# A three-pass fp32 transformer kernel: matmul order in the paired product, and one weight split moved ahead of a sigmoid

## The chip, the cores and the metric
One core of a Trainium2 chip runs the whole program. The metric is the device time of one execution in microseconds (us); lower is better.

## The reference
Four transformer layers over 256 tokens of width 1024, in fp32. Layer 0 mixes tokens by latent attention, layer 1 by dilated attention, layers 2 and 3 by a mixture of retention, block attention and a short convolution. Each layer ends with a gated feed-forward network of inner width 2816. Layers 0 and 1 then add a second, gated input. What matters here, cut down:

```
def swiglu(h, w_in, w_out):
    gu = h @ w_in                       # 1024 -> 2 x 2816
    return (jax.nn.silu(gu[..., :D_FF]) * gu[..., D_FF:]) @ w_out
...
h = h + rms_norm(swiglu(rms_norm(h, g[2]), ffn_w_in[i], ffn_w_out[i]), g[3])
h = h + (p[i] @ ple_w_proj[i]) * jax.nn.sigmoid(h @ ple_w_gate[i])   # layers 0 and 1
```

In layers 2 and 3 the feed-forward network has a short convolution and a GELU in the place of the SiLU.

## The kernel before
**Precision by three products.** Every fp32 operand is held as a high part and a low part (`w_hi` and `w_lo`, `xt_hi` and `xt_lo`), both as fp32r. A product is hi x hi + hi x lo + lo x hi, summed in PSUM.

**The stream of weights.** All weights come from HBM in chunks of at most 128 x 2048 numbers, numbered c through the whole program, into six slots (`SLOTS`). SP issues the load of chunk c when chunk c - 6 has been used (`chunk_used`). ScalarE makes the high part of each (L1057, `hi_part`), GpSimd subtracts it to get the low part (L440), and TensorE waits for that (`lo_split`) before its first matmul on the chunk. ScalarE has other work too, so its program says by hand where the high parts are made: `ahead(c, LEAD)` makes all high parts up to chunk c + 4 that are not made yet. An engine takes its instructions in the order written, so whatever stands behind a waiting high part waits too.

**The paired product** (`paired_product`, L547 to L558) computes 256 features of the feed-forward input (128 of each of its two matrices) from one chunk. There are 22 such chunks in a layer; the first three (layers 0 and 1) or four (layers 2 and 3) are computed in another way, the rest by `paired_product`. It has two halves of 128 features, one PSUM bank each. `xt_both` holds the high and the low part of the activations side by side, so one wide matmul of 512 columns gives hi x hi and hi x lo; a narrow one of 256 columns adds lo x hi to the first 256 columns. With eight pieces of the contraction (`kt`), a half has 8 wide and 8 narrow matmuls. Before, they run as 7 wide, 8 narrow, 1 wide. Every matmul has a weight load of its own.

**The end of layers 0 and 1** (`ple`). The gate projection has four chunks (C_GATE to C_GATE + 3), the second input's projection has one (C_PROJ = C_GATE + 4), and the next stage starts at C_GATE + 5. Rows are in two blocks of 128 tokens, tb 0 and tb 1. TensorE's order is: the first three gate chunks for tb 0 and for tb 1, the fourth for tb 0 (`gate0_ready`), the projection for tb 0 (`y0_ready`), the fourth gate chunk for tb 1 (`chunk_used`), the transposes of `h` for tb 0 (L617), the projection for tb 1, and then the next layer's first products. ScalarE takes the sigmoid of each block from PSUM into `t1` (L1177); VectorE multiplies the projection by it (L1659) and adds it to `h` (L1660), half a row block at a time; the transposes wait for each half (`rows_ready`).

**ScalarE's part before:** the high parts up to C_GATE + 6, then the wait for `gate0_ready` and the first sigmoid, then the high part of C_GATE + 7 (this is the third chunk of the next stage), then the wait for the second sigmoid.

Of the kernel before, what the change touches and what calls it, by code (L numbers as in the profile page):

```python
# [20 lines left out]
KT = D // P  # L21
# [6 lines left out]
LEAD = 4  # L28
# [24 lines left out]
PROJ_N, FFN_OUT_N = KT // 2, FT // 2  # L53
# [28 lines left out]
C_GATE = tuple(c + FFN_OUT_N for c in C_OUT[:2])  # L82
# [62 lines left out]
def build(nc, x, pT, positions, inv_freq, gain_fm, gain_rows, onehot, rel_table, rel_table_2, causal, decay,  # L145
# [7 lines left out]
    with ctx:  # L153
        def sb(name, shape, dt=F32, at=ctx):
            return at.enter_context(nc.sbuf_tensor(name, shape, dt))
# [11 lines left out]
        xt_both = sb("xt_both", [P, 2, KT, SEQ], F32R)  # L167
        xt_hi, xt_lo = xt_both[:, 0], xt_both[:, 1]
# [277 lines left out]
        def _(pe):  # L446
            def mm(dst, lhsT, rhs, start, stop):
                return nc.tensor.matmul(dst, lhsT, rhs, start=start, stop=stop)  # L448
# [13 lines left out]
            def chunk(c, cols):  # L462

                if c >= C_MLA:
                    pe.wait_ge(lo_split, c + 1 - C_MLA)
                s = c % SLOTS
                n = W // cols
                return (w_hi[:, s, 0:n * cols].rearrange("p (k n) -> p k n", n=cols),
                        w_lo[:, s, 0:n * cols].rearrange("p (k n) -> p k n", n=cols))
# [77 lines left out]
            def paired_product(c, banks):  # L547

                hi, lo = chunk(c, 2 * P)
                for half in range(2):  # L550
                    f = slice(half * P, (half + 1) * P)
                    both = psum[:, banks[half], :].rearrange("p (a t) -> p a t", a=2)
                    for kt in range(KT - 1):
                        mm(both, hi[:, kt, f], xt_both[:, :, kt, :], kt == 0, False)
                    for kt in range(KT):
                        mm(both[:, 0], lo[:, kt, f], xt_hi[:, kt, :], False, False)
                    ins = mm(both, hi[:, KT - 1, f], xt_both[:, :, KT - 1, :], False, True)
                ins.then_inc(chunk_used, 1)  # L558

            def wide_chunk(c, m, n, lhs, at, down=False, second=lambda: None):  # L560
# [68 lines left out]
            def ffn(l):  # L629

                t = T_FFN[l]
                held = BEGUN[t]

                def hidden_tile(u):
                    k = u - held
                    if k > 0:
                        pe.wait_ge(hidden_ready, l * FT + (1, held)[k - 1] if k < LANES else l * FT + u - LANES + 1)
                    paired_product(C_IN[l] + u, PAIRS_AT[k % LANES])

                def then():  # L640
                    if l < 2:
                        turn_r((2, 4)[l], t)
                    hidden_tile(held)

                begin_tiles(t, C_IN[l], then)
                for u in range(held + 1, FT):
                    hidden_tile(u)
                for m in range(FFN_OUT_N - HOLD):
                    pe.wait_ge(hidden_ready, l * FT + 2 * m + 2)
                    wide_chunk(C_OUT[l], m, FFN_OUT_N, (ht_hi, ht_lo), y_at("out", l),  # L650
                               second=(lambda: pe.wait_ge(hidden_ready, l * FT + FT - 2)) if m == 0 else lambda: None)
                pe.wait_ge(hidden_ready, l * FT + FT)
                wide_end(C_OUT[l], FFN_OUT_N, (ht_hi, ht_lo), y_at("out", l), (T_PLE0, T_PLE1, T_MIX3, None)[l], l >= 2)
# [282 lines left out]
            for l in (2, 3):  # L936
# [32 lines left out]
                for f in range(RH):  # L969
                    for tb in range(TB):  # L970
                        off = 2 * BANK + f * SEQ + tb * P
                        ins = nc.tensor.transpose(flat[:, off:off + P], ret[:, tb, f * P:(f + 1) * P], ident[:, :])
# [6 lines left out]
                for hh in range(RH):  # L979
# [3 lines left out]
                    ins = mm(logits[:, hh, far], q[:, P:SEQ], k, True, True)  # L983
# [7 lines left out]
                for hh in range(RH):  # L991
# [3 lines left out]
                    ins = mm(logits[:, hh, far], k[:, 0:P], q, True, True)  # L995
# [6 lines left out]
                for hh in range(RH):  # L1002
# [4 lines left out]
                    ins = mm(psum[:, 3, o], dec[:, hh, near], v[1], False, True)  # L1007
# [3 lines left out]
                for j in range(3 * RH):  # L1011
# [3 lines left out]
                    ins = nc.tensor.transpose(flat[:, off:off + P], sc2[:, j // 3, (j % 3) * P:(j % 3 + 1) * P], ident[:, :])  # L1015
# [7 lines left out]
                for hh in range(RH):  # L1023
# [4 lines left out]
                    ins = mm(flat[rows, off + P:off + SEQ], mvr[:, 1, hh, :], probT2[:, 3 * hh + 2, :], False, True)  # L1028
# [22 lines left out]
        def _(act):  # L1051
            def hi_part(c):

                s = c % SLOTS
                act.wait_ge(landed[s], 16 * (c // SLOTS + (1 if s >= C_MLA else 0)))
                width = WIDTHS[c]
                nc.scalar.activation(w_hi[:, s, 0:width], raw[:, s, 0:width], ACT.Copy).then_inc(hi_split, 1)  # L1057
# [3 lines left out]
            def ahead(c, lead=2):  # L1061

                while begun[0] < min(c + lead + 1, CHUNKS):
                    hi_part(begun[0])
                    begun[0] += 1
# [34 lines left out]
            def border(t, y, c, normed):  # L1100

                held = BEGUN.get(t, 0)

                for tb in range(TB):
                    if y is not None:
                        y_squares(y, tb)
                    if tb == 1:
                        ahead(c, LEAD)
                        copy_rows(t, 0, range(held - 2))
                    turn_hi_block(t, xt_hi, tb)  # L1110
                    if normed:
                        act.wait_ge(rows_ready, rows_of(t, tb, 1))
                        h_squares(tb)
                ahead(c + 1, LEAD)
                copy_rows(t, 0, range(max(held - 2, 0), held))
                ahead(c + 2, LEAD)
                copy_rows(t, 1, range(held if t == T_DIL else min(held, 2)))
# [48 lines left out]

            def ple(l, then):

                for m in range(PROJ_N - 1):
                    ahead(C_GATE[l] + m, LEAD)  # L1170
                for tb in range(TB):
                    if tb == 0:
                        act.wait_ge(gate0_ready, l + 1)
                    else:
                        ahead(C_GATE[l] + PROJ_N - 1, LEAD)
                        act.wait_ge(chunk_used, C_PROJ[l])
                    nc.scalar.activation(t1[:, tb, :], flat[:, 2 * tb * BANK:(2 * tb + 2) * BANK],  # L1177
                                         ACT.Sigmoid).then_inc(sig_ready, 1)
                border(then, None, C_PROJ[l], then == T_DIL)
# [141 lines left out]
            load_gain(2, 0)  # L1321
            ffn(0)
            ple(0, T_DIL)
            load_gain(3, 1)

# [74 lines left out]
            load_gain(4, 0)  # L1400
            ffn(1)
            ple(1, T_MIX2)
            load_gain(5, 1)


            for l in (2, 3):
# [8 lines left out]
                for b in range(3):  # L1415
# [4 lines left out]
                    for tb in range(TB):  # L1420
                        src = psum[:, b % 2 + 2 * tb, :]
                        if b < 2:
                            ins = nc.scalar.activation(ret[:, tb, b * BANK:(b + 1) * BANK], src, ACT.Copy)
                        else:
                            nc.scalar.activation(ret[:, tb, 2 * BANK:3 * RW], src[:, 0:split], ACT.Copy)
                            ins = nc.scalar.activation(ret[:, tb, 3 * RW:], src[:, split:], ACT.Silu)
                    ins.then_inc(ret_copied, 1)
                for b in range(3):
                    ahead(c + 6 + b, LEAD - 1)
                    act.wait_ge(chunk_used, c + 7 + b)  # L1430
                    ins = nc.scalar.activation(mqk[:, b].rearrange("p a t -> p (a t)"), psum[:, 5 + b, :], ACT.Copy)
# [8 lines left out]
                for tb in range(TB):  # L1440
                    ins = nc.scalar.activation(mvr[:, tb, :, :].rearrange("p h d -> p (h d)"), psum[:, tb, 0:RW], ACT.Copy)
# [3 lines left out]
                for m in range(2 * RH):  # L1445
                    part = sc2[:, m % RH, near if m < RH else far]
                    ins = nc.scalar.activation(part, part, ACT.Exp, bias=nmax[:, m:m + 1], accum_out=rsum[:, m:m + 1])
# [645 lines left out]
```

## Time and profile before

| | |
|---|---|
| median of 3 runs | 1490.85 us (1490.66 to 1492.28) |
| profiled execution, its own time | 1492.28 us |
| its span in the profile | 1490.5 us |
| granted TensorE clock | 0.997 of full speed |
| busy: TensorE, GpSimd, ScalarE, VectorE | 97%, 71%, 48%, 44% |

Rows give times from the start of the span. PE is TensorE's matmuls and PEld its weight loads, DVE is VectorE, ACT is ScalarE, POOL is GpSimd, SPq the DMA issues of SP. The length of a matmul in the rows overlaps with its neighbours', so the pace of a stream is read from the starts.

### The profile page before, as it was taken

The numbers are of one execution on the slowest core, as the hardware profiler recorded it, in microseconds if no ns is written. First come the engines' busy times: TensorE is split into PE (matmuls) and PEld (weight loads), VectorE is DVE, ScalarE is ACT, GpSimd is POOL, SyncE is SP. The second block draws the span as 40 slices with busy tenths as digits, with TensorE's granted clock in tenths as the row PEclk, the third lists the DMA queues.
The fourth block names the chain that finished last, engine by engine and source line by source line (L and its number), as shares of the span: only waits on it lengthen the run. The fifth ranks groups of instructions, "written<-read, shape, count | busy, mean of one in ns | idle before, by whom it ended". The sixth has DMA issues, their size and how long they took to land.

```text
span 1490.5 us, 22190 instructions
## 1 busy us (share of the span) xinstructions
PE 1452.9 (97%) x9070; PEld 1291.8 (87%) x9070; DVE 651.9 (44%) x1346; ACT 714.8 (48%) x920; POOL 1058.4 (71%) x262
## 2 busy tenths in 40 slices
PE   7899999999999999999999999999999999999997
PEld 6788888889999999888888889889888899898885
DVE  5545545033322222345541335646660475556613
ACT  6775555344544444465544345535443346255540
POOL 4366988965566665568888668768889577678891
PEclk9999999999999999999999999999999999999999
DMA  6475555545554554435555465336556555355560
GB/s 224 160 279 194 177 191 197 191 165 193 177 180 160 176 172 159 170 118 208 197 184 189 167 249 199 123 137 213 188 197 221 185 207 190 123 198 187 183 224 29
DMA packets 64670, 271.19 MB, mean 182 GB/s; under 512 B 6122, under 2 KB 28832, under 8 KB 37953
## 3 DMA queue, kind: packets, MB, share of 16 engines
q1 hardware_dynamic: 39596, 242.22, 46.9%
q10 hardware_dynamic: 24981, 27.61, 5.5%
q8 instruction: 72, 1.18, 0.3%
q14 instruction: 21, 0.17, 0.0%
HBM read 268.68 MB, written 8.21 MB: 186 GB/s over the span
## 4 chain that ended last, share of the span: by engine, by line
PE 91%; DVE 5%; ACT 2%; issue 1%; DMA 0%; SPq 0%; DVEq 0%
PE psum L448 87%; PE psum L617 1%; PE psum L864 1%; DMA h<-x 0%; PE psum L526 0%; ACT prob L1274 0%; DVE prob L1763 0%; DVE newton L1509 0%; DVE psum L1668 0%; DVE psum L1678 0%; ACT xt_both L1075 0%; DVE nmax L1765 0%; DVE xt_both L1593 0%; ACT probT L1280 0%; DVE rstd L1512 0%
## 5 line engine op out<-in xcount | busy, mean ns | idle before, releaser
L440 POOL TENSOR_TENSOR w_lo<-raw,w_hi 128x2048 fp32r<-128x2048 f32 (+2 forms) x248 | 1045.0, 4230 | 391.9 <-ACT w_hi L1057 391.5
L1057 ACT ACTIVATE w_hi<-raw 128x2048 fp32r<-128x2048 f32 (+2 forms) x248 | 433.5, 1754 | 146.8 <-DMA raw<-w_tail 88.3
L448 PE MATMUL psum<-xt_both,w_hi 128*128 128x512 f32 (+1 forms) x2272 | 498.0, 341 | 0.8 <-DVE dqk L1811 0.8
L448 PEld LDWEIGHTS psum<-xt_both,w_hi 128*128 128x128 f32 x2272 | 382.1, 190 | 44.9 <-issue 6.0
L448 PE MATMUL psum<-w_hi,xt_both 128*128 128x256 f32 (+3 forms) x1328 | 318.4, 329 | 1.4 <-DVE xt_both L1593 1.4
L448 PE MATMUL psum<-xt_both,w_lo 128*128 128x256 f32 x1728 | 318.9, 282 | 0.0
L448 PEld LDWEIGHTS psum<-xt_both,w_lo 128*128 128x128 f32 x1728 | 265.6, 191 | 11.6
L448 PEld LDWEIGHTS psum<-w_hi,xt_both 128*128 128x128 f32 x1328 | 229.1, 190 | 18.1 <-issue 3.8
L448 PE MATMUL psum<-w_lo,xt_both 128*128 128x256 f32 (+3 forms) x664 | 211.0, 326 | 0.0
L448 PEld LDWEIGHTS psum<-w_lo,xt_both 128*128 128x128 f32 x664 | 126.1, 190 | 7.1
L1145 ACT ACTIVATE lanes<-lanes 128x256 f32<-128x256 f32 x88 | 36.8, 418 | 166.6 <-DVE lanes L1630 107.9
L448 PE MATMUL psum<-w_hi,ht_hi 128*128 128x512 f32 x352 | 108.7, 390 | 0.0
L448 PE MATMUL psum<-w_lo,ht_hi 128*128 128x512 f32 x352 | 108.5, 389 | 0.0
L448 PE MATMUL psum<-w_hi,ht_lo 128*128 128x512 f32 x352 | 108.3, 389 | 0.0
L1619 DVE TENSOR_TENSOR psum<-psum,rest 128x512 f32<-128x512 f32 x74 | 51.8, 700 | 108.8 <-ACT rest L1142 108.8
L448 PEld LDWEIGHTS psum<-w_lo,ht_hi 128*128 128x128 f32 x352 | 66.1, 188 | 13.8
L448 PEld LDWEIGHTS psum<-w_hi,ht_lo 128*128 128x128 f32 x352 | 66.1, 188 | 13.8
L448 PEld LDWEIGHTS psum<-w_hi,ht_hi 128*128 128x128 f32 x352 | 65.9, 188 | 13.3
L1142 ACT ACTIVATE rest<-psum 128x512 f32<-128x512 f32 x74 | 43.4, 587 | 50.4 <-PE psum L448 50.4
L1352 ACT ACTIVATE prob<-prob,nmax 128x384 f32<-128x384 f32 (+1 forms) x32 | 24.7, 773 | 67.5 <-DVE nmax L1824 67.5
L1668 DVE SCALAR_TENSOR_TENSOR psum<-h,psum 128x1024 f32<-128x1024 f32 x8 | 9.8, 1229 | 106.7 <-PE psum L448 106.6
L1562 DVE TENSOR_TENSOR psum<-psum,gbuf 128x512 f32<-128x512 f32 x16 | 11.1, 695 | 100.3 <-ACT lanes L1083 100.3
(212 smaller groups left out, 1389.2 us busy)
## 6 DMA issues: line engine op xcount, KB each, us to landing
raw<-w_tail SPq DMA_DIRECT2D x156, 1024.0 KB, 4.9
raw<-w_dil SPq DMA_DIRECT2D x24, 1024.0 KB, 4.9
raw<-w_mix SPq DMA_DIRECT2D x24, 1024.0 KB, 5.0
raw<-w_dil SPq DMA_DIRECT2D x16, 576.0 KB, 3.7
bias_tiles<-bias_rows ACTq DMA_DIRECT2D x1, 6912.0 KB
gbuf<-gain_rows ACTq DMA_DIRECT2D x12, 512.0 KB, 5.0
dbias<-bias_tiles ACTq DMA_DIRECT2D x16, 384.0 KB, 6.1
raw<-w_dil SPq DMA_DIRECT2D x8, 384.0 KB, 4.5
```

The costliest lines, as they stand in the source:

```text
L440: nc.gpsimd.tensor_tensor(w_lo[:, s, 0:width], raw[:, s, 0:width], w_hi[:, s, 0:width].bitcast(F32), ALU.subtract).then_inc(lo_split, 1)
L448: return nc.tensor.matmul(dst, lhsT, rhs, start=start, stop=stop)
L617: ins = nc.tensor.transpose(psum[:, bank, n * P:(n + 1) * P], src[:, tb, kt * P:(kt + 1) * P], ident[:, :])
L864: ins = nc.tensor.transpose(flat[:, 5 * BANK + j * P:5 * BANK + (j + 1) * P], prob1[:, j * P:(j + 1) * P], ident[:, :])
L1057: nc.scalar.activation(w_hi[:, s, 0:width], raw[:, s, 0:width], ACT.Copy).then_inc(hi_split, 1)
L1142: nc.scalar.activation(rest[:, k], psum[:, first:first + 2, SEQ:2 * SEQ], ACT.Copy).then_inc(rest_ready, 1)
L1145: nc.scalar.activation(gate[:, u % LANES, :], conv[:, u % LANES, :], func).then_inc(gate_ready, 1)
L1352: nc.scalar.activation(prob1[:, part], prob1[:, part], ACT.Exp, bias=nmax[:, qb:qb + 1], accum_out=rsum_q[:, qb, hh:hh + 1]).then_inc(d_ex ...
L1562: return v.tensor_tensor(rows[:, cols], rows[:, cols], gbuf[:, slot, cols], ALU.mult)
L1619: step(v.tensor_tensor(both, both, rest[:, k], ALU.add))
L1668: step(v.scalar_tensor_tensor(rows, h[:, tb, :], ALPHA, rows, ALU.mult, ALU.add))
```

## The change
In `paired_product` the wide and the narrow matmuls of a half alternate by `kt`, and the last wide one stays last. In ScalarE's part of `ple` the high part of chunk C_GATE + 7 moves from behind the first sigmoid to ahead of the wait for it.

```
--- before
+++ after
@@ paired_product (TensorE)
-                    for kt in range(KT - 1):
-                        mm(both, hi[:, kt, f], xt_both[:, :, kt, :], kt == 0, False)
                     for kt in range(KT):
-                        mm(both[:, 0], lo[:, kt, f], xt_hi[:, kt, :], False, False)
-                    ins = mm(both, hi[:, KT - 1, f], xt_both[:, :, KT - 1, :], False, True)
+                        if kt < KT - 1:
+                            mm(both, hi[:, kt, f], xt_both[:, :, kt, :], kt == 0, False)
+                        ins = mm(both[:, 0], lo[:, kt, f], xt_hi[:, kt, :], False, False)
+                    ins = mm(both, hi[:, kt, f], xt_both[:, :, kt, :], False, True)
@@ ple (ScalarE)
-                for m in range(PROJ_N - 1):
+                for m in range(PROJ_N):
                     ahead(C_GATE[l] + m, LEAD)
                 for tb in range(TB):
                     if tb == 0:
                         act.wait_ge(gate0_ready, l + 1)
                     else:
-                        ahead(C_GATE[l] + PROJ_N - 1, LEAD)
                         act.wait_ge(chunk_used, C_PROJ[l])
```

PROJ_N is 4, KT is 8, TB is 2.

## Rows read from the trace of the kernel before

**Rows 1.** The page: busy times, and the chain that ended last by engine.

```profile
PE 1452.9 (97%) x9070; PEld 1291.8 (87%) x9070; DVE 651.9 (44%) x1346; ACT 714.8 (48%) x920; POOL 1058.4 (71%) x262
...
PE 91%; DVE 5%; ACT 2%; issue 1%; DMA 0%; SPq 0%; DVEq 0%
```

**Rows 2.** Groups of instructions by shape, TensorE; busy us, mean ns of one.

```profile
L448 PE MATMUL psum<-xt_both,w_hi 128*128 128x512 f32 x1184 | 298.5, 393 | 0.0
```

**Rows 3.** Timeline of paired halves, layer 0, TensorE: start, length, what.

```profile
202.25 1.11 PE L448 MATMUL psum<-xt_both,w_lo 128*128 128x256 f32 x8
203.20 2.00 PE L448 MATMUL psum<-xt_both,w_hi 128*128 128x512 f32 x8
...
203.67 0.39 PE L448 MATMUL psum<-xt_both,w_hi 128*128 128x512 f32 x1
203.90 0.40 PE L448 MATMUL psum<-xt_both,w_hi 128*128 128x512 f32 x1
...
205.04 1.11 PE L448 MATMUL psum<-xt_both,w_lo 128*128 128x256 f32 x8
...
205.04 0.30 PEld L448 LDWEIGHTS psum<-xt_both,w_lo 128*128 128x128 f32 x2
```

**Rows 4.** Timeline, TensorE: a stretch of 512 columns, one of 256 columns.

```profile
320.53 0.87 PEld L448 LDWEIGHTS psum<-w_hi,xt_both 128*128 128x128 f32 x4
...
323.25 0.87 PEld L448 LDWEIGHTS psum<-w_hi,xt_both 128*128 128x128 f32 x4
...
341.28 0.28 PE L448 MATMUL psum<-w_lo,xt_both 128*128 128x256 f32 x1
...
343.80 0.28 PE L448 MATMUL psum<-w_lo,xt_both 128*128 128x256 f32 x1
```

**Rows 5.** Tile view of `raw`, layer 0: issue and landing of chunk C_GATE + 7.

```profile
L390 SPq DMA_DIRECT2D raw<-w_dil x1: 328/328/328, 326.8 to 326.8; - x1
...
DMA to landing us min/median/max: 5.0/5.0/5.0
```

**Rows 6.** Timeline, end of layer 0, ScalarE and GpSimd.

```profile
330.93 1.28 ACT L1177 ACT_TABLE_LOAD   x1
330.99 9.19 POOL L440 TENSOR_TENSOR w_lo<-raw,w_hi 128x2048 fp32r<-128x2048 f32 x2 [0.68 <-ACT w_hi L1057]
...
332.28 1.03 ACT L1177 ACTIVATE t<-psum 128x1024 f32<-128x1024 f32 x1
...
333.21 1.91 ACT L1057 ACTIVATE w_hi<-raw 128x2048 fp32r<-128x2048 f32 x1
...
337.73 1.02 ACT L1177 ACTIVATE t<-psum 128x1024 f32<-128x1024 f32 x1 [2.61 <-PE psum L448]
```

**Rows 7.** Timeline, end of layer 0, VectorE and TensorE's transposes.

```profile
335.07 0.70 DVE L1659 TENSOR_TENSOR psum<-psum,t 128x512 f32<-128x512 f32 x1 [15.10 <-PE psum L448]
...
337.14 0.69 DVE L1660 TENSOR_TENSOR h<-psum,h 128x512 f32<-128x512 f32 x1
...
337.30 1.02 PEld L617 LDWEIGHTS psum<-ident,h 128*128 128x128 f32 x8
...
344.69 0.42 PEld L617 LDWEIGHTS psum<-ident,h 128*128 128x128 f32 x4 [0.30 <-DVE h L1660]
```

**Rows 8.** Tile view of `raw`, layer 1: issue and landing of chunk C_GATE + 7.

```profile
L390 SPq DMA_DIRECT2D raw<-w_mix x1: 328/328/328, 855.4 to 855.4; - x1
...
DMA to landing us min/median/max: 6.4/6.4/6.4
```

**Rows 9.** Timeline, end of layer 1, ScalarE.

```profile
861.27 1.28 ACT L1177 ACT_TABLE_LOAD   x1
862.56 1.03 ACT L1177 ACTIVATE t<-psum 128x1024 f32<-128x1024 f32 x1
```

**Rows 10.** Timeline, end of layer 1, VectorE and TensorE's transposes.

```profile
863.68 0.70 DVE L1659 TENSOR_TENSOR psum<-psum,t 128x512 f32<-128x512 f32 x1 [15.11 <-ACT t L1177]
...
865.91 1.02 PEld L617 LDWEIGHTS psum<-ident,h 128*128 128x128 f32 x8
```

## The prediction, on record before the changed kernel ran

> **What bounds the kernel now.** I read the page first: TensorE is busy for 97% of the span and is 91% of the chain that ended last [rows 1]. A matmul saved or lengthened there is therefore worth its full time, and so is any pause of TensorE. Then I read the groups by shape, to count what the first edit touches: 1184 matmuls of 512 columns (weights `w_hi`, moving `xt_both`) [rows 2]. They are 74 paired chunks (19, 19, 18 and 18 in the four layers) of two halves with 8 each, so 148 halves, and each half has 8 narrow matmuls of 256 columns with `w_lo` as well. The "busy" time of a row is no help for the price, since matmuls overlap; I go by the distance from one start to the next. Last I read the timeline of each engine at the end of layers 0 and 1, where `ple` runs, for the second edit.
>
> **The first edit: the order of matmuls in `paired_product`.** Nothing is added or removed: each half has the same 8 wide and 8 narrow matmuls, the same loads, bank and semaphores, and the chunk's wait stands at its start as before. Only the sequence changes, from 7 wide, 8 narrow, 1 wide to wide, narrow, wide, narrow and so on, with two narrow ones side by side near the end. Switches from narrow to wide go from 1 to 7 in a half, and as many from wide to narrow.
>
> What does a half take now? Eight wide ones start at 203.20 and the narrow ones behind them at 205.04: 1.84 us. The eight narrow ones before them run from 202.25 to 203.20: 0.95 us. A half is 2.79 us [rows 3]. What would both kinds take at their settled distance? In the gate projection, where all are 512 wide, 12 matmuls (loads of 2, 4, 2 and 4) go from 320.53 to 323.25, so 0.2267 us each; in the first products of the dilated layer, all 256 wide, 21 go from 341.28 to 343.80, so 0.120 us each [rows 4]. Eight of both are 2.77 us. So the present order costs about 0.02 us a half over the settled distances, and the narrow ones are not starved: 0.95 for eight is what they take in a stretch of their own. There is no large pool of time for the new order to collect; 148 times 0.02 is 3 us.
>
> A rule of the Trainium skill speaks against a gain too. "TensorE: Matmul & The Clock Gate", section "LDWEIGHTS (loading the stationary operand)", gives a load as its columns over 1.2, which for 128 columns makes an estimate of 107 ns; by it the load is already hidden behind a narrow matmul and needs no wide one before it. The trace agrees in so far as the narrow ones go on at 0.120 us for as long as they last [rows 4].
>
> What could a switch itself cost? The trace has no stream that alternates the two, so I bound it by the matmuls just behind a switch. Wide after narrow: the first starts at 203.20, the third at 203.67 and the fourth at 203.90, so 0.235 us each over the first two and 0.233 over three, against 0.2267 settled. Narrow after wide: two loads begin at 205.04 and end 0.30 later, of which the second takes 0.19, so it began at 205.15, with the second narrow matmul: 0.11 us after the first, against 0.120 [rows 3].
> - Bad end: each wide one costs 0.235 and each narrow one its settled 0.120. A half is 8 x 0.235 + 8 x 0.120 = 2.84, which is +0.05, or +7.4 us in all.
> - Good end: wide ones stay at 0.2267 and each narrow one behind a wide costs 0.115 (between 0.11 and 0.12). 8 x 0.2267 + 7 x 0.115 + 0.12 = 2.74, which is -0.05, or -8 us.
> - Between them: wide 0.233 with narrow 0.115 gives 2.79, no change; both at their settled distance give 2.77, -3 us.
> The last two are nearest to what the rows show of a single switch, so I take the region between them, -2 us.
>
> **The second edit: in `ple`, the high half of one more chunk is made before the first sigmoid.** `ahead(C_GATE+3, 4)` splits chunk C_GATE+7, the third chunk of the stage that follows (four gate chunks and one projection chunk lie between). It used to come after the first sigmoid, now it comes before it. The work is the same, but ScalarE takes its queue in order, so the table load, the sigmoid of rows 0 to 127, VectorE's multiply and add, and TensorE's transposes of `h` now stand behind this chunk's landing.
>
> Layer 0. The DMA is issued at 326.8 and lands 5.0 later, at 331.8 [rows 5]. ScalarE was free at 330.93, where it started the table load, so it now waits 0.9 us, then copies for 1.9 us (to 333.7), loads the table, and starts the sigmoid 1.35 us later as it did before (330.93 to 332.28): at 335.1 in place of 332.28 [rows 6]. Before, that was hidden: the sigmoid ended at 333.31 and VectorE started at 335.07, when the projection's product was there. Now the sigmoid ends at about 336.2, so VectorE starts 1.2 late. Its four steps end 2.76 us after their start (337.14 + 0.69 - 335.07), at 337.83 before; TensorE's eight transposes began to load at 337.30 and were at the fifth, the first that needs the second half of these rows, at about 337.8 (eight in 1.02 us) [rows 7]. So TensorE has no slack there, and stops for 1.2 us. At its next turn it had waited 0.30 us for `h` [rows 7]; that wait is now met by TensorE's own lateness, so 0.9 us remain. The second sigmoid is not late: its start at 337.73 is set by TensorE's product ahead of the transposes [rows 6].
>
> Layer 1. The DMA is issued at 855.4 and lands 6.4 later, at 861.8 [rows 8]. The copy runs to 863.7, the sigmoid starts 1.3 later (861.27 to 862.56 before) at 865.05 in place of 862.56 [rows 9]: 2.5 us late. Here there was no cover: VectorE started at 863.68, with the end of the sigmoid. Its second half ended 2.76 later at 866.44, and TensorE's transposes loaded from 865.91, so the fifth was due at 866.4 [rows 10]. TensorE stops for 2.5 us, and up to the next layer's first products the view of the waits shows none of TensorE's that could take it up.
>
> What does it give? The copy of this chunk ends earlier (333.7 for 335.1 in layer 0), but GpSimd, which needs it, was at the chunk before it until 335.6 (two in 9.19 us from 330.99) [rows 6]. It gains nothing. Behind the late transposes stand the projection's second block and its `chunk_used`, and on SP one stream load, of a chunk that ScalarE reads microseconds later. Sum of the edit: 0.9 + 2.5 = +3.4 us.
>
> **The sum** is -2 + 3.4 = +1.4 us. The profiled execution took 1492.28 us, 1.8 more than its span of 1490.5; with the change this would be 1493.7. It is the slowest of the three runs, so I put the 1.4 on the median, 1490.85: 1492.3 us.
>
> **The rivals.**
> - The order is worth the good end. For it: the narrow ones behind a wide one do start closer together. Against it: only the first does. -8 + 3.4 = -4.6: 1486.2 us. The skill's page has a rule on this side: its section "Back-to-back issue gap" says that spacing is set by load and matmul together through a queue that lets loads be pulled forward, so a wide matmul would lend its slack to the load behind the narrow one. In this trace a load starts with the matmul before it and no earlier (both rows of 205.04) [rows 3].
> - Slower by the order: each switch to wide costs what the first two wide ones cost now, and the narrow ones give nothing back. Its place is the 1184 wide matmuls; +7.4 + 3.4 = +10.8: 1501.7 us. It decides once a wide one takes over 0.2315 us with narrow ones at 0.120 (then a half is 2.81 and the sum passes +6).
> - The second edit does nothing to the end: the chunk lands early enough, or the late transposes are absorbed by waits that I don't see. The landings speak against it. -2: 1488.9 us.
> - The order is worth nothing or costs a little (2.79 to 2.81 a half) and the sigmoids are late: +3.4 to +6: 1494.3 to 1497 us.
>
> **How the numbers follow.** 0.2% of this time, 3 us, is about what a measurement of this kernel tells from no change. Chances: my forecast (+0.4 to +3.4) 0.45; good end 0.2; bad end 0.1; second edit without effect 0.12; order worth nothing and sigmoids late 0.13. The forecast is itself "same" but for a small part at its upper end. The good end is mostly "faster". The fourth is mostly "same". The last and the bad end are "slower". That makes 0.2 faster, 0.47 same, 0.33 slower. The range runs from the good end to near the bad one, and leaves out half of the latter and a little below the former: 1486 to 1499 us. The likeliest case's own range is 1491 to 1494.5.
>
> **What would show it.** In a paired half, the distance from a run's first wide start to the next half's: 2.78 means that the order is neutral, 2.74 the good end, 2.84 the bad one. At the end of layers 0 and 1 ScalarE's row of L1057 should start at the landing (about 5.0 and 6.4 after the issue), the sigmoid 2.8 and 2.5 later than before against the product that it reads, and TensorE should show idle time before the transposes with VectorE's `h` as its releaser, 1.2 and 2.5 us. I am wrong if that idle time is missing, or if alternating matmuls settle to a distance that neither kind shows beside its own.

## The result, and the profile after

The changed kernel takes 1500.17 us (median of 5 runs, 1497.27 to 1503.59) where the kernel before took 1490.85 in the runs beside it: a ratio of 1.0058, with a 95% interval of 1.0039 to 1.0078. Measured once more (`after_again` below) it gave 1499.89 us against 1493.52, 1.0041 (1.0027 to 1.0055). It is slower by about half a per cent; 1492.3 was predicted and 1499 was the upper end of the range.

The page of the changed kernel, its busy times and its chain (the lines that answer to [rows 1]):

```profile
span 1500.9 us, 22190 instructions
...
PE 1460.5 (97%) x9070; PEld 1292.8 (86%) x9070; DVE 652.2 (43%) x1346; ACT 715.3 (48%) x920; POOL 1057.3 (70%) x262
...
PE 90%; DVE 5%; ACT 3%; DMA 1%; issue 1%; SPq 0%; DVEq 0%
```

The same number of instructions, 22190, stands in a longer span, and the chain has more of ScalarE and DMA in it (3% and 1%, where it had 2% and 0%). As both kernels issue 9070 matmuls and only their order within a half differs, the start of the n-th matmul can be set against the start of the n-th before. The distance between the two grows by 3.9 us over the four feed-forward stretches (1.0, 1.0, 0.95 and 0.95), by 0.6 at the end of layer 0, by 4.5 at the end of layer 1, by 1.6 near 644 us and by 1.6 near 972, and shrinks by 1.6 near 1270 us. That is 10.6; all else takes back about 0.1, and the spans differ by 10.4. Lines 1176, 1658 and 1659 of the changed kernel are lines 1177, 1659 and 1660 of the kernel before.

**The order.** Timeline of paired halves of the changed kernel, TensorE (answers to [rows 3]):

```profile
175.49 0.63 PE L448 MATMUL psum<-xt_both,w_hi 128*128 128x512 f32 x2
175.96 0.28 PE L448 MATMUL psum<-xt_both,w_lo 128*128 128x256 f32 x1
176.07 0.39 PE L448 MATMUL psum<-xt_both,w_hi 128*128 128x512 f32 x1
...
176.42 0.40 PE L448 MATMUL psum<-xt_both,w_hi 128*128 128x512 f32 x1
...
177.83 0.40 PE L448 MATMUL psum<-xt_both,w_hi 128*128 128x512 f32 x1
...
178.31 0.63 PE L448 MATMUL psum<-xt_both,w_hi 128*128 128x512 f32 x2
```

A half takes 178.31 - 175.49 = 2.82 us in place of 2.79. Five pairs of one wide and one narrow matmul run from 176.07 to 177.83, 0.352 us a pair. The settled distances of [rows 4] add up to 0.347.

**The late sigmoid.** Timeline at the end of layer 1, ScalarE, VectorE and the weight loads of TensorE's transposes (answers to [rows 9, 10]):

```profile
864.32 1.92 ACT L1057 ACTIVATE w_hi<-raw 128x2048 fp32r<-128x2048 f32 x1 [8.79 <-DMA raw<-w_mix]
866.84 1.92 ACT L1057 ACTIVATE w_hi<-raw 128x2048 fp32r<-128x2048 f32 x1 [0.61 <-DMA raw<-w_mix]
868.78 1.28 ACT L1176 ACT_TABLE_LOAD   x1
870.07 1.94 ACT L1176 ACTIVATE t<-psum 128x1024 f32<-128x1024 f32 x2
871.13 0.70 DVE L1658 TENSOR_TENSOR psum<-psum,t 128x512 f32<-128x512 f32 x1 [18.47 <-ACT t L1176]
...
872.61 0.44 PEld L617 LDWEIGHTS psum<-ident,h 128*128 128x128 f32 x4 [2.66 <-DVE h L1659]
...
873.94 0.71 PEld L617 LDWEIGHTS psum<-ident,h 128*128 128x128 f32 x4 [0.89 <-DVE h L1659]
```

And the tile view of `raw` there, the chunk's issue and landing (answers to [rows 8]):

```profile
L390 SPq DMA_DIRECT2D raw<-w_mix x1: 328/328/328, 859.5 to 859.5; - x1
...
DMA to landing us min/median/max: 7.3/7.3/7.3
```

Begin with the landing. The chunk is issued at 859.5 and lands 7.3 later; ScalarE copies it from 866.84, loads the table, takes the sigmoid at 870.07; VectorE starts at 871.13; TensorE idles 2.66 us for the first half of `h` and 0.89 for the second, 3.5 in all. VectorE's start in [rows 10], moved by the 4.1 us that had gathered by then, would be 867.8: it is 3.4 us late.

Not all of this is the edit's. The first row is the copy of chunk C_GATE + 6, which stands ahead of the first sigmoid in both kernels. It starts at 864.32, as soon as that chunk has landed, and ends at 866.24; even with the `ple` of before the table could not have been loaded sooner. In the kernel before the same copy started at 859.33:

```profile
859.33 1.92 ACT L1057 ACTIVATE w_hi<-raw 128x2048 fp32r<-128x2048 f32 x1 [7.88 <-DMA raw<-w_mix]
```

Moved by the 4.1 us this is 863.4, so the late landing of C_GATE + 6 alone would have made VectorE some 0.9 us late. The moved copy, which put the table load at 868.78 in place of 866.26, adds the other 2.5.

The same place in layer 0 (answers to [rows 7]):

```profile
338.43 0.42 PEld L617 LDWEIGHTS psum<-ident,h 128*128 128x128 f32 x4 [0.25 <-DVE h L1659]
339.76 0.42 PEld L617 LDWEIGHTS psum<-ident,h 128*128 128x128 f32 x4 [0.91 <-DVE h L1659]
```

That is 1.16 us of waiting, and the wait of 0.30 at the next transposes is gone.

**The clock.** Windows of the changed kernel at the end of layer 1; columns are the window, its length, PE busy with the number of its matmuls, PEclk (the granted clock), DMA share and GB/s:

```profile
865.00:885.00 20.00, 17.26 (x74) 0.91 0.38 135
873.10:876.50 3.40, 2.90 (x11) 0.52 0.37 154
```

For 3.4 us, from between the two parts of that wait on, TensorE was granted about half of its clock (0.52 over this window), which is the level of 1.2 GHz in place of 2.4. Such a stretch is called a half-clock period below. The trace of the changed kernel has three of them before its last 10 us (from 644, 873 and 972 us); that of the kernel before has one, from 1269 us. In this row PEld, DVE, ACT and POOL stand between PE busy and PEclk, which is 0.50:

```profile
1269.30:1272.70 3.40, 3.40 (x9) 2.62 (x8) 0.44 (x1) 0.00 (x0) 3.40 (x2) 0.50 0.02 5
```

Those from 644 and 972 us and the one of the kernel before make the steps of 1.6, 1.6 and -1.6 in the list above; the one from 873 us makes about 0.9 of the 4.5 at the end of layer 1, where TensorE was idle for a part of it.

### The profile page after: what moved, and what is told of

It reads as the page before. It is cut to its first block, busy times and chain, and to the rows that moved or that the text cites. A ratio compares the mean times of both kernels' runs of the same rounds, so it can differ in the third digit from the quotient of the medians.

```text
span 1500.9 us, 22190 instructions
## 1 busy us (share of the span) xinstructions
PE 1460.5 (97%) x9070; PEld 1292.8 (86%) x9070; DVE 652.2 (43%) x1346; ACT 715.3 (48%) x920; POOL 1057.3 (70%) x262
## 4 chain that ended last, share of the span: by engine, by line
PE 90%; DVE 5%; ACT 3%; DMA 1%; issue 1%; SPq 0%; DVEq 0%
PE psum L448 86%; PE psum L617 1%; PE psum L864 1%; ACT w_hi L1057 1%; DMA raw<-w_mix 0%; PE psum L526 0%; DMA h<-x 0%; ACT prob L1273 0%; DVE prob L1762 0%; DVE newton L1508 0%; DVE psum L1667 0%; DMA raw<-w_dil 0%; DVE psum L1677 0%; DVE nmax L1764 0%; DVE rstd L1511 0%
## 5 line engine op out<-in xcount | busy, mean ns | idle before, releaser
L448 PE MATMUL psum<-xt_both,w_hi 128*128 128x512 f32 (+1 forms) x2272 | 607.9, 344 | 0.8 <-DVE dqk L1810 0.8
L448 PE MATMUL psum<-xt_both,w_lo 128*128 128x256 f32 x1728 | 462.0, 281 | 0.0
L448 PEld LDWEIGHTS psum<-xt_both,w_lo 128*128 128x128 f32 x1728 | 327.7, 190 | 13.6
```

## The experiments

All ran beside runs of the kernel before on the same chip. Three chips were used, with 1492.49, 1492.56 and 1493.52 us as the medians of before, so each version is set against its own. `runs4`, `runs2` and `all_wide_alt` ran once each (1494.57, 1493.49 and 1616.72 us) and are read by their traces and not by these times.

### Each edit by itself

`order_only` has the new loop of `paired_product` and the `ple` of before. `split_only` is the reverse.

```
# order_only: the paired_product of the change; ple as before
# split_only: paired_product as before; in ple
-                for m in range(PROJ_N - 1):
+                for m in range(PROJ_N):
...
-                        ahead(C_GATE[l] + PROJ_N - 1, LEAD)
```

> Only the order of the matmuls in the paired product is changed. In the changed kernel a paired half took 2.825 us against 2.798 (means over 148), which is 4.0 us. Theory S (each switch between narrow and wide costs time of its own): halves at 2.825 again, no new idle time of TensorE, +4 us, a ratio of 1.0026, plus whatever the number of half-clock periods (3.4 us each, some 1.5 us lost in each) differs by. Rival (the slow halves come from the late chunks of the other edit or from the clock): halves back at 2.80, ratio 1.000. Theory C (the added half-clock periods follow from the new idle time at the end of layers 0 and 1): here none at 870 to 880 us.

Measured: 1496.01 us (8 runs) against 1492.49 (20 runs), ratio 1.0028 (1.0018 to 1.0038). In its trace the ends of layers 0 and 1 are as before, and the feed-forward stretches add 3.9 us again. It has no half-clock period near 870 us, as theory C expects. One row of the chain shows it best: TensorE runs from 150.5 us in layer 0 through 828 matmuls without a pause, 36 paired halves among them. First the kernel before:

```profile
150.51 157.71 PE psum L448 x828
```

and the same row of `order_only`:

```profile
150.51 158.65 PE psum L448 x828
```

0.94 us over 36 halves is 0.026 each; times 148 it is 3.9 us. The order costs this with neither late chunks nor clock behind it, as theory S says; whether the cost goes by the number of switches is the question of the next section.

> Only the high part of chunk C_GATE + 7 is moved ahead of the first sigmoid. TensorE should wait for h before the transposes at the end of layer 0 (1.2 us in all) and of layer 1 (3.6 us over two waits, as in the changed kernel), the order left as it was, halves at 2.798. Sum at full clock: 0.6 + 2.8 = +3.4 us, ratio 1.0023. Theory C: a half-clock period shortly after the wait in layer 1, near 870 us, which adds some 1.5 us, so +5 us and 1.0033. Rival: the wait only moves other waits and is given back by the end, ratio 1.000.

Measured: 1497.62 us (6 runs) against 1492.49, ratio 1.0033 (1.0021 to 1.0045). Its trace has +0.7 at the end of layer 0, near the 0.6 of the changed kernel, but only +0.9 at the end of layer 1. The tile view of `raw` and the timeline of `split_only` there:

```profile
L390 SPq DMA_DIRECT2D raw<-w_mix x1: 328/328/328, 856.3 to 856.3; - x1
...
DMA to landing us min/median/max: 4.8/4.8/4.8
```

```profile
865.39 0.70 DVE L1658 TENSOR_TENSOR psum<-psum,t 128x512 f32<-128x512 f32 x1 [15.97 <-ACT t L1176]
...
866.87 0.47 PEld L617 LDWEIGHTS psum<-ident,h 128*128 128x128 f32 x4 [0.16 <-DVE h L1659]
...
868.20 0.42 PEld L617 LDWEIGHTS psum<-ident,h 128*128 128x128 f32 x4 [0.86 <-DVE h L1659]
```

The chunk landed after 4.8 us here, against 6.4 in [rows 8] and 7.3 in the changed kernel, and so did chunk C_GATE + 6; TensorE waited 1.0 us in place of 3.5. Slack behind a landing that hid this before is used up by the moved copy, so the landing now comes through to the time, and it varies from one execution to the next. The expected 3.6 us of waiting and the half-clock period near 870 were both missing in this trace; its half-clock periods are at other places (966 and 1273 us). The two edits alone add 0.0028 and 0.0033. Their sum of 0.0061 agrees, within the intervals, with the 0.0058 of the change.

### How the order costs

> The order of before, with the wide matmuls of both halves of a chunk first, then the narrow ones of both, then the two last wide ones: one change from narrow to wide for each chunk instead of two. Theory S: a chunk of before has two runs at about 0.02 us over the settled distances (2.793 against 2.773 for a half by medians), so 0.02 us less for each of 74 chunks, a chunk at 5.57 us against 5.59, -1.5 us, ratio 0.999. Rival (the alternation itself, not the switch, is what costs, or two banks in turn cost more): no gain or a loss.

```
-                for half in range(2):
-                    f = slice(half * P, (half + 1) * P)
-                    both = psum[:, banks[half], :].rearrange("p (a t) -> p a t", a=2)
+                halves = []
+                for half in range(2):
+                    halves.append((slice(half * P, (half + 1) * P),
+                                   psum[:, banks[half], :].rearrange("p (a t) -> p a t", a=2)))
+                for f, both in halves:
                     for kt in range(KT - 1):
                         mm(both, hi[:, kt, f], xt_both[:, :, kt, :], kt == 0, False)
+                for f, both in halves:
                     for kt in range(KT):
                         mm(both[:, 0], lo[:, kt, f], xt_hi[:, kt, :], False, False)
+                for f, both in halves:
                     ins = mm(both, hi[:, KT - 1, f], xt_both[:, :, KT - 1, :], False, True)
```

Measured: 1491.62 us (11 runs) against 1492.49, ratio 0.9993 (0.9984 to 1.0002), so the time alone does not tell it from before. The trace does. The row of the chain in `once_per_chunk`:

```profile
150.28 157.38 PE psum L448 x828
```

and two chunks of its timeline:

```profile
199.79 3.82 PE L448 MATMUL psum<-xt_both,w_hi 128*128 128x512 f32 x16
203.44 2.08 PE L448 MATMUL psum<-xt_both,w_lo 128*128 128x256 f32 x16
205.35 3.82 PE L448 MATMUL psum<-xt_both,w_hi 128*128 128x512 f32 x16
```

157.38 is 0.33 less than before over 18 chunks, 0.018 for each, which is 1.3 us over 74; a chunk is 205.35 - 199.79 = 5.56 us. As expected, one change of width less returns the 0.02.

> Four wide, four narrow, three wide, four narrow, one wide in each half: two switches from narrow to wide a half, where before has one and the changed kernel seven. If every switch costs the same 0.0045 us (0.027 over six more), a half takes 2.802 us. If what costs is the group of up to five wide matmuls behind each switch (their distances sum to about 0.025 over the settled ones), two such groups cost twice as much as one: 2.82 us, as much as the seven switches of the changed kernel. Read from the trace, 148 halves.

```
-                    for kt in range(KT - 1):
-                        mm(both, hi[:, kt, f], xt_both[:, :, kt, :], kt == 0, False)
-                    for kt in range(KT):
-                        mm(both[:, 0], lo[:, kt, f], xt_hi[:, kt, :], False, False)
+                    for part in (range(0, 4), range(4, 8)):
+                        for kt in part:
+                            if kt < KT - 1:
+                                mm(both, hi[:, kt, f], xt_both[:, :, kt, :], kt == 0, False)
+                        for kt in part:
+                            mm(both[:, 0], lo[:, kt, f], xt_hi[:, kt, :], False, False)
```

> Runs of two wide and two narrow matmuls, four switches from narrow to wide a half where before has one, runs of four two and the changed kernel seven. The means were 2.798 (one), 2.801 (two) and 2.825 (seven). A cost for each switch of 0.0044 us gives 2.811; if only the strict alternation of single matmuls costs, it stays at 2.80.

`runs2` has parts of two pieces in place of four. The row of the chain, `runs4` and then `runs2`:

```profile
150.82 157.81 PE psum L448 x828
```

```profile
150.64 158.40 PE psum L448 x828
```

Over the 157.71 of before this is +0.10 and +0.69 us, 0.003 and 0.019 a half. So with one, two, four and seven changes from narrow to wide a half, the cost over before is 0, 0.003, 0.019 and 0.026 us. It rises with every step, but not by an equal amount: the group theory (0.02 for two changes) is out, and 0.0044 a change is too high for the second and too low for the next two. What sets the price of each change is not shown.

> The changed kernel's alternating order with every low-weight matmul made 512 columns wide as well (low weights times both parts of the activations), so that w_hi and w_lo take turns as weights but the width never changes. It adds the product low x low to the result, and 8 x 0.107 us of columns to a half. If the change of width is what costs, a half takes 16 x 0.2267 = 3.627 us, its distances all at 0.227. If the turn of the weights from one tensor to the other is what costs, the distances stay at about 0.235 and a half takes 3.77 us.

```
 # on the changed kernel's loop
-                        ins = mm(both[:, 0], lo[:, kt, f], xt_hi[:, kt, :], False, False)
+                        ins = mm(both, lo[:, kt, f], xt_both[:, :, kt, :], False, False)
```

The timeline of `all_wide_alt`:

```profile
202.72 0.39 PE L448 MATMUL psum<-xt_both,w_lo 128*128 128x512 f32 x1
202.95 0.39 PE L448 MATMUL psum<-xt_both,w_hi 128*128 128x512 f32 x1
...
204.99 0.39 PE L448 MATMUL psum<-xt_both,w_lo 128*128 128x512 f32 x1
```

Ten matmuls from 202.72 to 204.99, 0.227 us each, the settled distance of [rows 4]. Taking turns between the two weight tensors is free; taking turns between the two widths is not. With the width, the part of `xt_both` that is read and the part of the PSUM bank that is written change too; no run separates these.

### The late sigmoid, the landing and the clock

> The order of before, with two high parts moved ahead of the first sigmoid, chunks C_GATE + 7 and C_GATE + 8. The second has its slot 2.7 us later, so the sigmoid waits for a later landing. In layer 1: issue near 859, landing 4.8 to 7.4 later at 864 to 866, copy 1.9, table 1.3, so VectorE starts 3 to 4 us later than with one chunk moved and TensorE waits 4 to 6 us for h; in layer 0 about 1.2 us more than with one. Full-clock sum +6 to +9 us. If long idle time of TensorE brings half-clock periods, one stands near 870 us in the profile and the granted clock of the timed runs lies below that of one chunk moved (mean 0.9955); if these periods fall without regard to it, the clock stays at 0.9955 to 0.9964 and the time at +6 to +9.

```
-                for m in range(PROJ_N - 1):
+                for m in range(PROJ_N + 1):
                     ahead(C_GATE[l] + m, LEAD)
...
-                        ahead(C_GATE[l] + PROJ_N - 1, LEAD)
```

Measured: 1501.66 us (5 runs) against 1492.56 (15 runs), ratio 1.0058 (1.0045 to 1.0072). Timeline of `split_two` at the end of layer 1, the loads of the transposes, and its windows there (columns as above):

```profile
870.99 0.42 PEld L617 LDWEIGHTS psum<-ident,h 128*128 128x128 f32 x4 [2.75 <-DVE h L1659]
872.32 0.71 PEld L617 LDWEIGHTS psum<-ident,h 128*128 128x128 f32 x4 [0.91 <-DVE h L1659]
```

```profile
865.00:885.00 20.00, 17.00 (x73) 0.91 0.30 105
```

TensorE waits 3.7 us, less than the 4 to 6 expected; the chunks landed early here, after 4.7 and 4.8 us. A half-clock period begins at 871.7. The mean granted clock of its runs is 0.9936, the lowest of all, against 0.9961 for before beside it.

> The changed kernel once more, beside the others on one chip. By parts: order +3.9 us, late sigmoids +1.5 to +3.5 us by the landing in layer 1 (4.8 to 7.4 us), and 1.4 us for each 0.001 by which the mean granted clock is below that of before. Sum +6.5 to +9.5 us, ratio 1.0045 to 1.0063. If the first measurement was high by chance alone, it is the two edits without the clock: 1.0036 to 1.005.

Measured: 1499.89 us (5 runs) against 1493.52 (21 runs), 1.0041 (1.0027 to 1.0055), mean clock 0.9948 against 0.9961. The ratio is a little below the range that was expected for the two edits with the clock, and inside the one without it. The loads of its transposes in layer 1, and its windows:

```profile
870.87 0.42 PEld L617 LDWEIGHTS psum<-ident,h 128*128 128x128 f32 x4 [2.11 <-DVE h L1659]
872.20 0.72 PEld L617 LDWEIGHTS psum<-ident,h 128*128 128x128 f32 x4 [0.91 <-DVE h L1659]
```

```profile
865.00:885.00 20.00, 17.63 (x76) 0.91 0.30 108
```

It waits 3.0 us, with the landing after 6.7, and has a half-clock period from 871.6.

> The second edit in layer 0 alone. TensorE waits 1.2 us for h there, gives 0.5 back at the next wait, +0.65 us, and layer 1 is as before, with no wait before its transposes. Theory C (half-clock periods come with the long wait in layer 1): the granted clock is that of before, 0.9963, and the ratio 1.0004. Rival (any short wait brings one): clock near 0.9955 and a ratio near 1.002.

```
-                for m in range(PROJ_N - 1):
+                for m in range(PROJ_N if l == 0 else PROJ_N - 1):
                     ahead(C_GATE[l] + m, LEAD)
```

Measured: 1492.54 us (11 runs) against 1493.52, ratio 0.9995 (0.9986 to 1.0004), mean clock 0.9969. Its trace has +0.55 us at the end of layer 0 and 0.4 at the end of layer 1, and the window there shows the full clock. The wait in layer 1 was not expected, since `ple` is there as before; chunk C_GATE + 6 had landed after 7.0 us, and its copy alone made the first sigmoid late:

```profile
869.96 0.42 PEld L617 LDWEIGHTS psum<-ident,h 128*128 128x128 f32 x4 [0.38 <-DVE h L1660]
```

```profile
865.00:885.00 20.00, 19.85 (x97) 1.00 0.37 129
```

The edit in layer 0 can't be told from nothing by its time, though the traces show its 0.6 us. The larger part of the cost lies in layer 1.

What do the traces say together of the clock near 870 us? Three have a wait of 3.0 us or more before the transposes of layer 1 (the changed kernel twice, `split_two`), and all three have a half-clock period that begins within it, in its second part or between the two. None of the nine others with this layout has one there; their waits are 0 to 1.0 us. At three places TensorE idles in every one of these twelve traces: 1.9 us near 643, and 2.0 near 966 and near 1270 us. This is the wait of the kernel before ahead of its period from 1269 us:

```profile
1268.09 0.70 PE L448 MATMUL psum<-w_hi,ot_hi 128*128 128x512 f32 x2 [2.00 <-DVE ot_lo L1931]
```

A half-clock period follows in four, six and seven of the twelve traces at these places and is missing in the rest. So waits of some 2 us bring one in about half of the cases, and the three long ones in layer 1 did each time. That the wait is the cause is argued from this pattern; what decides for one execution is not shown. The periods are plain in the times: of 21 executions of before beside `after_again`, the nine at a clock of 0.997 took 1490.4 to 1492.4 us and the twelve at 0.995 or 0.996 took 1493.0 to 1494.7.

### A version that beats both

> One change of width a chunk (as in the kernel with one switch a chunk, -18 ns for each of 74, -1.3 us) and the second edit turned round: the high parts of C_GATE + 6 and C_GATE + 7 both come after the first sigmoid, so that it never waits for a landing. In the runs where chunk C_GATE + 6 lands at 6.4 us or later in layer 1 the sigmoid is 1 to 2 us earlier, but VectorE needs the projection too, which is done at the same time: at most 0.3 us at the end of layer 1 when the landing is late, nothing in layer 0. GpSimd starts the low part 2 us later, with slack before TensorE needs it at 872. Sum -1.3 to -1.8 us, ratio 0.9990. Rival: the low parts come late, TensorE waits for lo_split after the transposes, and it is slower.

```
 # with paired_product of once_per_chunk
-                for m in range(PROJ_N - 1):
+                for m in range(PROJ_N - 2):
                     ahead(C_GATE[l] + m, LEAD)
...
-                        ahead(C_GATE[l] + PROJ_N - 1, LEAD)
+                        for m in range(PROJ_N - 2, PROJ_N):
+                            ahead(C_GATE[l] + m, LEAD)
```

Measured: 1490.92 us (11 runs) against 1492.56 (15 runs), ratio 0.9987 (0.9978 to 0.9996). It is the only one whose interval lies below 1. Its mean clock was 0.9967 against 0.9961, so part of the 1.6 us can be the clock.

> The order of before, and both high parts (C_GATE + 6 and C_GATE + 7) made after the first sigmoid. In the traces so far TensorE never waits for the first sigmoid when one high part stands ahead of it, so nothing is gained: ratio 1.000 within 0.001, and the gain of the kernel that has this and one change of width a chunk (0.9987) belongs to the order of matmuls. Rival: late landings in some executions make it worth up to 0.5 us, ratio 0.9997, which these rounds cannot tell apart from nothing.

The paired product is that of before, and `ple` that of `chunk_and_later`.

Measured: 1492.01 us (11 runs) against 1493.52, ratio 0.9993 (0.9984 to 1.0002). Neither half of that version is clear of no change by itself. The order's 1.3 us is seen in the traces; that the later copies are worth anything is not shown. They can only help in an execution where C_GATE + 6 lands late, as in the trace of `split_layer0` (0.4 us); in the trace of before TensorE had no wait there to remove.

## Why the prediction was wrong

**What bounds the kernel: right.** TensorE sets the end, and what both edits did to it came through to the time.

**The price of the order: the step that failed.** The text says of no change and of -3 us that they are "nearest to what the rows show of a single switch", and takes -2 us from between them. The runs show +3.9. The bounds were good (-8 to +7.4); the choice between them was not. It took the narrow matmul behind a switch at 0.115 and let a wide one settle back to 0.2267 or stay at 0.233. In an alternating stream none settles: the pair takes 0.352 us, a wide one at 0.235 (two in 0.47 from 175.49) and a narrow one at 0.117, near the "second wide" rows from which the bad end was made. The sign had been in the text: the present order was found 0.02 us a half above the settled distances, with one change of width. That is a price for a change of width, and the edit makes seven; `once_per_chunk` confirms it from the other side. It gave the sign and not the size: six more changes cost 0.026 us a half, not six times 0.02. The Trainium skill ("TensorE: Matmul & The Clock Gate", "LDWEIGHTS (loading the stationary operand)") gives a load as its columns over 1.2, which makes an estimate of 107 ns for 128 columns. The rows of the loads are longer, 0.19 us each in the groups of both traces, yet narrow matmuls with a load each start every 0.120 us. So what the prediction took from it, no large gain, holds, and no run bears out the rival that a wide matmul lends its slack to the next load.

**The late sigmoids: right in mechanism and place, with one term read as fixed that is not.** Layer 0: 1.2 us of wait forecast, 1.16 measured; 0.9 us of it left forecast, 0.6 measured, since besides the wait of 0.30 a pause of 0.2 us just before it is gone. Layer 1: 2.5 forecast from a landing after 6.4 us. In the changed kernel VectorE was 3.4 us late, 2.5 by the moved copy and 0.9 by the landing of C_GATE + 6, which the forecast did not look at; in `split_only`, where both chunks landed after 4.8 us, it was 0.9 late. The landings of one trace stood for all. The second sigmoid was not to be late by itself; in layer 1 of the changed kernel it follows the first without a gap at 870.07, which changed nothing. That GpSimd gains nothing holds.

**Left out: the clock.** Two more half-clock periods in the changed kernel's trace than in that of before, about 2.5 us of its 10.4, have no term in the sum. By the mean clocks it is 0.0013 less than before (`after_again`), some 2 us. The one in layer 1 is, by the pattern above, a second price of the wait.

**The range.** The bad end of the order alone, with the sigmoids, was 1501.7 us, and half of it was cut away. The rival "slower by the order" named the mechanism and sized it at +7.4 where it is +3.9. With 1.5 to 4.1 us for the sigmoids (the traces of `split_only` and of the changed kernel) and 2 for the clock it makes 7.4 to 10. The medians differ by 9.3 us in the first measurement, inside this, and by 6.4 in the second, which is 1 us below it and not explained. The likeliest case held the sigmoids alone.

## What to carry to other kernels

Count the changes of width in a stream of matmuls, and compare the stream with its settled distances: what it loses now with few changes gives the sign of what it will lose with many, though not the size. Before a copy is moved ahead of something on the path, look up when its data lands, in more than one execution, and what stands in line behind it: here a wait that had been free was put in front of a sigmoid, and the idle time of TensorE behind it ran from 1.0 to 3.5 us. When TensorE is the bound, an idle stretch can cost more than its length.

## What the runs showed of the hardware that was not expected

- Wide (512 columns) and narrow (256) fp32r matmuls in turn take 0.352 us a pair, 0.005 over their settled distances of 0.227 and 0.120. Alternating weights at one width costs nothing (0.227).
- The load of the same chunk at the same place landed after 4.8, 6.4, 6.7 and 7.3 us in the traces of `split_only`, the kernel before, `after_again` and the changed kernel.
- A wait of TensorE of 3.0 to 3.7 us went with 3.4 us at the 1.2 GHz level in three traces of three; waits up to 1.0 us at that place did not, in nine traces, and waits of 1.9 to 2.0 us at three other places did in 17 cases of 36.
